# A decoder trunk on one core: three adaLN chunks summed through a fold on VectorE, with fewer steps in three units

## The chip, the cores and the metric

The kernel runs on one core of a Trainium2 chip. The time is device microseconds of one execution. Three runs of the kernel before gave 2296.66, 2296.85 and 2297.17 us; the median is 2296.85. In the text PE or TensorE is the matmul engine, DVE or VectorE the vector engine, ACT or ScalarE the activation engine, POOL or GpSimd and SP or SyncE the two engines that here only issue transfers.

## The reference

A two-layer trunk for 256 tokens of width 2048. Layer 0 mixes tokens by attention with a forget bias (16 heads of 128), layer 1 by a gated convolution of width 3; each is followed by an MLP with squared ReLU. Every sub-layer is normalised, shifted and scaled, and added back through a gate. The shifts, scales and gates (adaLN) come from the vector c:

```python
c_act = jax.nn.silu(c)
for i in range(DEPTH):
    mod = c_act @ ada_w[i] + ada_b[i]
    sh_mix, sc_mix, g_mix, sh_mlp, sc_mlp, g_mlp = jnp.split(mod, N_MOD, axis=-1)
    h = modulate(rmsnorm(x, norm_mix[i]), sh_mix, sc_mix)
    ...
    x = x + g_mix[:, None, :] * mix
    h = modulate(rmsnorm(x, norm_mlp[i]), sh_mlp, sc_mlp)
    x = x + g_mlp[:, None, :] * sq_relu_mlp(h, mlp_w_up[i], mlp_w_down[i])
return rmsnorm(x, final_norm)
```

Here `ada_w` is 2 x 2048 x 12288 in float32 (201 MB), a matrix that is read once for a product with one vector.

## The kernel before, in words

**Units and pairs.** The big products are cut into units: one unit is a 2048 x 512 slab of a weight matrix, multiplied in 8 pairs of two 128-row chunks. Units 0 to 11 are q, k and v of the four groups of heads (unit u makes part u % 3 of group u // 3), units 12 to 15 are the attention's output projection, and the MLPs and the convolution follow. Each float32 operand is split into a high and a low half of the matmul's own format, and each product is three matmuls: high x high, high x low, low x high. For every pair ScalarE rounds the weights to `w_hi` (L916), and VectorE subtracts to get `w_lo` (L1444). Both halves have four buffers (`WR`). A `w_hi` may be written when TensorE has used the pair four before it (`split_used`), and TensorE waits for `w_lo` (`split_ready`). In the body of unit u, the split at place i makes the pair 8u + 4 + i, so the two split engines work half a unit ahead.

**adaLN steps.** Of each adaLN part (2048 columns) there are two chunks of 1024 columns. A chunk takes 16 steps: a tile of 128 rows x 1024 columns of `ada_w` arrives in one of four buffers `ada_raw`, by a transfer that GpSimd issues when the step four before is done, and VectorE multiplies it by one column of c and adds it to an accumulator (L1464; the first of a chunk, L1461, only multiplies). Two accumulators alternate, `acc` for even and `hb` for odd chunks. What is left is a sum over the 128 partitions, and it has two forms (`ada_sum`, L549):

- plain: 8 matmuls with 128 x 128 blocks of the accumulator as weights and a column of ones (L562), and one store of 128 x 8 (L1495);
- folded (`fold_acc`, L1476): VectorE transposes the accumulator in blocks of 32 x 32 (L1481) and reduces it to 128 x 32 (L1483); then a single matmul with the matrix `fold` gives the sums. For a gate it is L556 with a store of 32 x 32 (L1502); for a shift or scale it is L558, and its store is four instructions, one for each 32 partitions (L1491).

`FOLDED` lists the chunks of the second form.

**The order of work.** `PLAN_QKV`, made by `plan` from rows of 8 numbers, says how many steps VectorE does behind each of the 8 splits of units 0 to 15. The six chunks done there are 0 and 1 (shift of the first MLP), 2 and 5 (its scale), 3 and 4 (gate of the attention). Where a chunk ends, `sums_of` puts its sum behind the pair four places later on TensorE and its store one place after that on VectorE. The order of each engine is fixed; semaphores alone hold them together.

**The attention between.** In units 5, 8 and 11 (and in 6 for group 1) TensorE computes a group's scores (L743 to L747), VectorE takes the maxima (L1756 to L1765), ScalarE the exponentials (L1140), VectorE the reciprocal of the sums (L1769), ScalarE normalises (L1147), and TensorE turns the probabilities (L754 to L756). Scores need the low halves of q and k, which VectorE makes behind their units (L1794). From unit 12 on a finished unit is multiplied by its gate and added to the residual (L1853, L1856).

## Time and profile before

| what | value |
|---|---|
| median of 3 runs | 2296.85 us |
| profiled execution | 2296.28 us |
| its span, first to last instruction | 2294.3 us |
| mean granted TensorE clock | 0.997 of full speed |
| PE busy | 2252.3 us (98%) |
| PE weight loads busy | 1918.9 us (84%) |
| DVE busy | 1698.3 us (74%) |
| ACT busy | 1095.7 us (48%) |
| bytes moved | 615.71 MB, mean 268 GB/s |

The busy shares are means over stages with different limits. The stage of units 5 to 15 lies between about 187 and 480 us, the first MLP behind it. A busy PE is not PE at its peak, since matmuls are pipelined and their records overlap: the distance between starts is what one costs. The same holds, by about 0.09 us, for instructions of VectorE that follow at once.

### The profile page before, as it was taken

To read this page: it belongs to the slowest core of one execution; us is meant where nothing else is said; L and a number is where in the kernel's file an instruction comes from. 1 tells how busy PE (TensorE), PEld (TensorE's weight loads), DVE (VectorE), ACT (ScalarE), POOL (GpSimd) and SP (SyncE) were. 2 spreads that over 40 slices of the span, in tenths; PEclk is the share of its full clock that TensorE was granted. 3 is DMA by queue.
4 is the path that set the end of the run, shared out by engine and by line. 5 is a ranking of instruction groups with operands and counts; after the bars stand their busy time and mean duration, and the time that the engine had idled before them with its cause. 6 is when DMAs were issued, how large, how long until landed. Compare 5 with 4: busy or idle time off the path is not lost.

```text
span 2294.3 us, 30019 instructions
## 1 busy us (share of the span) xinstructions
PE 2252.3 (98%) x11688; PEld 1918.9 (84%) x11688; DVE 1698.3 (74%) x1642; ACT 1095.7 (48%) x1264; POOL 172.6 (8%) x339
## 2 busy tenths in 40 slices
PE   6999999999999999999999999999999999999998
PEld 5999998878888888888887888887888888888886
DVE  6888999968958957967977888866895555555555
ACT  4455454464435435435545444446443543543553
POOL 0001121101101101101100111100110000000000
PEclk9999999999999999999999999999999999999999
DMA  9987999959968968978966888855986556565563
GB/s 363 386 320 258 347 354 364 349 188 319 339 214 301 348 213 286 338 236 272 335 238 238 310 326 331 317 184 168 320 302 218 185 184 202 184 195 190 184 213 117
DMA packets 271812, 615.71 MB, mean 268 GB/s; under 512 B 15472, under 2 KB 15808, under 8 KB 271296
## 3 DMA queue, kind: packets, MB, share of 16 engines
q1 hardware_dynamic: 220480, 437.56, 55.6%
q0 software_dynamic: 46080, 167.79, 20.1%
q10 hardware_dynamic: 5120, 8.49, 1.1%
q8 instruction: 96, 1.57, 0.3%
q14 instruction: 36, 0.29, 0.0%
HBM read 611.66 MB, written 2.13 MB: 268 GB/s over the span
## 4 chain that ended last, share of the span: by engine, by line
PE 92%; DVE 3%; DMA 2%; issue 1%; ACT 1%; SPq 0%; ACTq 0%; DVEq 0%
PE ps L516 19%; PE ps L518 19%; PE ps L517 19%; PE ps L504 16%; PE ps L505 8%; PE ps L491 2%; PE ps L492 2%; PE ps L493 2%; DMA start_ring<-in_ada_w_dram 2%; DVE acc L1464 1%; DVE square_out L1464 0%; PE ps L596 0%; DVE h L1600 0%; PE ps L623 0%; PE ps L880 0%
## 5 line engine op out<-in xcount | busy, mean ns | idle before, releaser
L916 ACT ACTIVATE w_hi<-raw 128x1024 fp32r<-128x1024 f32 x721 | 762.6, 1060 | 961.6 <-PE ps L518 691.9
L1444 DVE TENSOR_TENSOR w_lo<-raw,w_hi 128x1024 fp32r<-128x1024 f32 x721 | 877.6, 1222 | 449.8 <-ACT w_hi L916 448.5
L504 PE MATMUL ps<-h,w_hi 128*128 128x512 f32 x1536 | 541.4, 398 | 0.0
L516 PE MATMUL ps<-w_hi,mid 128*128 128x512 f32 x1280 | 500.0, 391 | 0.0
L518 PE MATMUL ps<-w_lo,mid 128*128 128x512 f32 x1280 | 498.4, 389 | 0.0
L517 PE MATMUL ps<-w_hi,mid 128*128 128x512 f32 x1280 | 498.4, 389 | 0.0
L505 PE MATMUL ps<-h,w_lo 128*128 128x256 f32 x1536 | 430.5, 280 | 0.0
L504 PEld LDWEIGHTS ps<-h,w_hi 128*128 128x128 f32 x1536 | 288.6, 188 | 71.6 <-DVE w_lo L1444 0.6
L516 PE MATMUL ps<-w_hi,h 128*128 128x512 f32 x756 | 298.6, 395 | 6.7 <-DVE h L1600 5.3
L518 PE MATMUL ps<-w_lo,h 128*128 128x512 f32 x756 | 294.7, 390 | 0.0
L517 PE MATMUL ps<-w_hi,h 128*128 128x512 f32 x756 | 294.6, 390 | 0.0
L505 PEld LDWEIGHTS ps<-h,w_lo 128*128 128x128 f32 x1536 | 290.1, 189 | 0.2
L474 POOL DMA_DIRECT2D ada_raw<-in_ada_w_dram x320 | 169.1, 528 | 1527.6 <-DVE acc L1461 553.7
L518 PEld LDWEIGHTS ps<-w_lo,mid 128*128 128x128 f32 x1280 | 240.3, 188 | 50.2
L516 PEld LDWEIGHTS ps<-w_hi,mid 128*128 128x128 f32 x1280 | 240.3, 188 | 50.0 <-DVE w_lo L1444 0.4
L517 PEld LDWEIGHTS ps<-w_hi,mid 128*128 128x128 f32 x1280 | 240.4, 188 | 49.1
L1464 DVE SCALAR_TENSOR_TENSOR hb<-ada_raw,ca,hb 128x1024 f32<-128x1024 f32 x150 | 191.5, 1277 | 3.3 <-DMA ada_raw<-in_ada_w_dram 2.5
L1464 DVE SCALAR_TENSOR_TENSOR acc<-ada_raw,ca,acc 128x1024 f32<-128x1024 f32 x150 | 191.7, 1278 | 2.1 <-DMA ada_raw<-in_ada_w_dram 0.9
L516 PEld LDWEIGHTS ps<-w_hi,h 128*128 128x128 f32 x756 | 142.0, 188 | 39.0 <-issue 9.6
L518 PEld LDWEIGHTS ps<-w_lo,h 128*128 128x128 f32 x756 | 141.9, 188 | 30.1
L517 PEld LDWEIGHTS ps<-w_hi,h 128*128 128x128 f32 x756 | 142.1, 188 | 27.8
L491 PE MATMUL ps<-h,w_hi 128*128 128x256 f32 x512 | 148.1, 289 | 1.3 <-DVE h L1600 1.3
(246 smaller groups left out, 1801.4 us busy)
## 6 DMA issues: line engine op xcount, KB each, us to landing
ada_raw<-in_ada_w_dram POOLq DMA_DIRECT2D x320, 512.0 KB, 6.4
raw<-in_mlp_w_up_dram SPq DMA_DIRECT2D x128, 1024.0 KB, 5.3
raw<-in_mlp_w_down_dram SPq DMA_DIRECT2D x128, 1024.0 KB, 5.8
raw<-in_fox_w_in_dram SPq DMA_DIRECT2D x48, 1024.0 KB, 10.9
raw<-in_conv_w_in_dram SPq DMA_DIRECT2D x48, 1024.0 KB, 7.9
start_ring<-in_ada_w_dram SPq DMA_DIRECT2D x64, 512.0 KB, 12.2
raw<-in_fox_w_out_dram SPq DMA_DIRECT2D x16, 1024.0 KB, 10.1
raw<-in_conv_w_out_dram SPq DMA_DIRECT2D x16, 1024.0 KB, 5.1
```

The lines of the kernel that those rows point to most:

```text
L474: pool.dma_start(ada_raw[:, t % TILES, :], ada_tile(t // KC, t % KC)).then_inc(ada_arrived[t % TILES], 16)
L491: mm(o, hi[:, jc], xh, start=(k == first and j % 2 == 0), stop=False, skip_group_check=True)
L492: mm(o, hi[:, jc], xl, start=False, stop=False, skip_group_check=True)
L493: last = mm(o, lo[:, jc], xh, start=False, stop=(k == end - 1), skip_group_check=True)
L504: mm(o, hi[:, jc], both, start=(k == 0), stop=False, skip_group_check=True)
L505: last = mm(o[:, 0:T], lo[:, jc], rhs[:, k, 0, :], start=False, stop=(k == KC - 1), skip_group_check=True)
L516: mm(o, xh, hi, start=(k == first), stop=False)
L517: mm(o, xl, hi, start=False, stop=False)
L518: last = mm(o, xh, lo, start=False, stop=(k == end - 1))
L916: op(w_hi[:, e % WR], raw[:, e // 2, EK * (e % 2):EK * (e % 2 + 1)], ACT.Copy).then_inc(hi_ready, 1)
L1444: v.tensor_tensor(w_lo[:, e % WR], raw[:, e // 2, EK * (e % 2):EK * (e % 2 + 1)], w_hi[:, e % WR].bitcast(F32), ALU.subtract).then_inc(spl ...
L1464: v.scalar_tensor_tensor(slot, src, ca[:, col:col + 1], slot, ALU.mult, ALU.add).then_inc(steps, 1)
```

## The change

Chunks 0, 1 and 2 get the folded form; of the six chunks of these units only chunk 5 (the second half of the scale) stays plain. The plan takes 10 steps in place of 11 in units 6, 7 and 8, spread otherwise within the unit, and 6, 8, 8 in place of 4, 8, 7 in units 12, 13, 14. Total and order of the steps are the same: 96. Chunks end later, so sums and stores move: in pairs (unit, place) the sums go from (6, 6), (8, 2), (9, 6), (11, 1), (13, 2) to (6, 7), (8, 4), (10, 0), (11, 4), (13, 3). The sum of chunk 5 stays at (15, 2), now by a number written out. ScalarE's write and load of the second half of the first gate come one place later in unit 13.

```diff
--- before.py
+++ after.py
@@ -60,7 +60,7 @@
 A_MLP1 = A_CONV + 2 * NH
 A_END = A_MLP1 + NH
 BLK = 32
-FOLDED = [i for i, (b, _) in enumerate(ADA) if PARTS[b] in GATE or i >= A_MLP0]
+FOLDED = [i for i in range(len(ADA)) if i != A_MLP0 - 1]
 TILES = 4
 
 
@@ -88,7 +88,8 @@
 SIX = [1, 1, 1, 0, 1, 1, 1, 0]
 FIVE = [1, 1, 1, 1, 1, 0, 0, 0]
 HALF = [1, 0] * 4
-LATE = [0] * 4 + [1] * 4
+LATE = [0] * 4 + [2, 1, 2, 1]
+EVEN = [1, 1, 1, 2, 1, 1, 2, 1]
 NONE = [0] * 8
 
 
@@ -106,7 +107,7 @@
     return first, ends
 
 
-PLAN_QKV = plan([NONE] * N_START + [ELEVEN] * 7 + [LATE, DENSE, SEVEN, NONE])
+PLAN_QKV = plan([NONE] * N_START + [ELEVEN, EVEN, EVEN, EVEN, ELEVEN, ELEVEN, ELEVEN, LATE, DENSE, DENSE, NONE])
 PLAN_SLICE = plan([NONE, SIX, SIX, SIX, SEVEN, SEVEN, NONE, NONE])
 PLAN_CONV = plan([NONE, DENSE, SIX] + [HALF, DENSE, SIX] * 2 + [HALF, DENSE, [1, 1] + [0] * 6])
 
@@ -386,7 +387,7 @@
                 at_store[t] = i
             return at_sum, at_store
 
-        QKV_SUM, QKV_STORE = sums_of(PLAN_QKV)
+        QKV_SUM, QKV_STORE = sums_of(PLAN_QKV, {2 * NH + 1: (8 * U_OUT0 + 26, 8 * U_OUT0 + 27)})
         SLICE_SUM, SLICE_STORE = sums_of(PLAN_SLICE, {1: (PLAN_SLICE[1][1] + 3, PLAN_SLICE[1][1] + 4)})
         CONV_SUM, CONV_STORE = sums_of(PLAN_CONV)
 
@@ -1300,7 +1301,7 @@
             for n in range(NG):
                 residual(at(U_OUT0 + n), n, R_OUT0, 1,
                          ({4: lambda: gate_load(0, 0, 0)},
-                          {3: load_root, 4: lambda: gate_write(A_GATE0 + 1, 0, 1), 6: lambda: gate_load(0, 1, 0)}, None, None)[n],
+                          {3: load_root, 5: lambda: gate_write(A_GATE0 + 1, 0, 1), 7: lambda: gate_load(0, 1, 0)}, None, None)[n],
                          first=None if n else {0: lambda: round_probs(NG - 1), 4: lambda: round_attn(NG - 1)})
 
 
```

What moves on VectorE is shown at three places. In the rows below, line numbers of the new kernel are one higher (L1465 is L1464 of before).

VectorE in unit 7, from the end of group 1's maxima to its reciprocal, before:

```order
L1765 TENSOR_TENSOR exp_bias<-f_tok,row_max 128x8
L1464 SCALAR_TENSOR_TENSOR hb<-ada_raw,ca,hb 128x1024
L1794 SCALAR_TENSOR_TENSOR qs<-ps,qs 128x4x256
L1444 TENSOR_TENSOR w_lo<-raw,w_hi 128x1024
L1495 TENSOR_TENSOR mod<-ps,vcol 128x8
L1464 SCALAR_TENSOR_TENSOR hb<-ada_raw,ca,hb 128x1024
L1444 TENSOR_TENSOR w_lo<-raw,w_hi 128x1024
L1769 RECIPROCAL row_inv<-row_sum 128x8
```

and now:

```order
L1766 TENSOR_TENSOR exp_bias<-f_tok,row_max 128x8
L1465 SCALAR_TENSOR_TENSOR hb<-ada_raw,ca,hb 128x1024 x2
L1795 SCALAR_TENSOR_TENSOR qs<-ps,qs 128x4x256
L1445 TENSOR_TENSOR w_lo<-raw,w_hi 128x1024
L1465 SCALAR_TENSOR_TENSOR hb<-ada_raw,ca,hb 128x1024
L1445 TENSOR_TENSOR w_lo<-raw,w_hi 128x1024
L1492 TENSOR_TENSOR mod<-ps,vcol 32x8 x4
L1770 RECIPROCAL row_inv<-row_sum 128x8
```

One step more stands behind the maxima, and the store of chunk 0 is four instructions, directly ahead of the reciprocal.

VectorE from the low half of k of group 3 (unit 10's end) to that group's first row maxima in unit 11, before:

```order
L1794 SCALAR_TENSOR_TENSOR ks<-ps,ks 128x4x256
L1444 TENSOR_TENSOR w_lo<-raw,w_hi 128x1024
L1464 SCALAR_TENSOR_TENSOR acc<-ada_raw,ca,acc 128x1024
L1444 TENSOR_TENSOR w_lo<-raw,w_hi 128x1024
L1464 SCALAR_TENSOR_TENSOR acc<-ada_raw,ca,acc 128x1024 x2
L1444 TENSOR_TENSOR w_lo<-raw,w_hi 128x1024
L1464 SCALAR_TENSOR_TENSOR acc<-ada_raw,ca,acc 128x1024
L1444 TENSOR_TENSOR w_lo<-raw,w_hi 128x1024
L1502 TENSOR_TENSOR gate_parts<-ps,gate_parts 32x32
L1756 TENSOR_REDUCE row_max<-ps 128x4
```

and now:

```order
L1795 SCALAR_TENSOR_TENSOR ks<-ps,ks 128x4x256
L1445 TENSOR_TENSOR w_lo<-raw,w_hi 128x1024
L1465 SCALAR_TENSOR_TENSOR hb<-ada_raw,ca,hb 128x1024
L1445 TENSOR_TENSOR w_lo<-raw,w_hi 128x1024
L1465 SCALAR_TENSOR_TENSOR hb<-ada_raw,ca,hb 128x1024
L1482 STREAM_TRANSPOSE hb<-hb 128x1024
L1484 TENSOR_REDUCE acc_part<-hb 128x32
L1462 TENSOR_SCALAR acc<-ada_raw,ca 128x1024
L1445 TENSOR_TENSOR w_lo<-raw,w_hi 128x1024
L1465 SCALAR_TENSOR_TENSOR acc<-ada_raw,ca,acc 128x1024
L1445 TENSOR_TENSOR w_lo<-raw,w_hi 128x1024
L1757 TENSOR_REDUCE row_max<-ps 128x4
```

The transpose and reduction of chunk 3 now stand within this stretch; before they stood ahead of it (with the last step of the chunk before them). Between the maxima of group 2 in unit 8 and this low half of k there are 29 steps and one fold in both orders: chunk 3's before, chunk 2's now. Of the 29 steps two are the first of a chunk before, one now, and the stretch holds two plain stores before and two stores of four instructions now.

VectorE in unit 12, from the first step behind the split of pair (13, 0) to the w_lo of pair (13, 4), before:

```order
L1464 SCALAR_TENSOR_TENSOR acc<-ada_raw,ca,acc 128x1024
L1444 TENSOR_TENSOR w_lo<-raw,w_hi 128x1024
L1464 SCALAR_TENSOR_TENSOR acc<-ada_raw,ca,acc 128x1024
L1444 TENSOR_TENSOR w_lo<-raw,w_hi 128x1024
L1464 SCALAR_TENSOR_TENSOR acc<-ada_raw,ca,acc 128x1024
L1481 STREAM_TRANSPOSE acc<-acc 128x1024
L1483 TENSOR_REDUCE acc_part<-acc 128x32
L1853 TENSOR_TENSOR scratch<-ps,gate 128x1024
L1856 TENSOR_TENSOR xr<-xr,scratch 128x2x512
L1444 TENSOR_TENSOR w_lo<-raw,w_hi 128x1024
L1461 TENSOR_SCALAR hb<-ada_raw,ca 128x1024
L1444 TENSOR_TENSOR w_lo<-raw,w_hi 128x1024
```

and now:

```order
L1465 SCALAR_TENSOR_TENSOR acc<-ada_raw,ca,acc 128x1024 x2
L1445 TENSOR_TENSOR w_lo<-raw,w_hi 128x1024
L1465 SCALAR_TENSOR_TENSOR acc<-ada_raw,ca,acc 128x1024
L1445 TENSOR_TENSOR w_lo<-raw,w_hi 128x1024
L1465 SCALAR_TENSOR_TENSOR acc<-ada_raw,ca,acc 128x1024 x2
L1854 TENSOR_TENSOR scratch<-ps,gate 128x1024
L1857 TENSOR_TENSOR xr<-xr,scratch 128x2x512
L1445 TENSOR_TENSOR w_lo<-raw,w_hi 128x1024
L1465 SCALAR_TENSOR_TENSOR acc<-ada_raw,ca,acc 128x1024
L1482 STREAM_TRANSPOSE acc<-acc 128x1024
L1484 TENSOR_REDUCE acc_part<-acc 128x32
L1445 TENSOR_TENSOR w_lo<-raw,w_hi 128x1024
```

Two more steps stand ahead of the gated addition (`scratch<-ps,gate`), and the fold has gone from ahead of it to behind the split that follows it.

## Rows read from the trace of the kernel before

**Rows 1.** The page: busy time by engine, and the chain of waits.

```profile
PE 2252.3 (98%) x11688; PEld 1918.9 (84%) x11688; DVE 1698.3 (74%) x1642; ACT 1095.7 (48%) x1264; POOL 172.6 (8%) x339
...
PE 92%; DVE 3%; DMA 2%; issue 1%; ACT 1%; SPq 0%; ACTq 0%; DVEq 0%
```

**Rows 2.** Windows: us, busy of PE, PEld, DVE, ACT, POOL; PEclk, DMA share, GB/s.

```profile
290.00:360.00 70.00, 70.00 (x517) 66.81 (x516) 67.44 (x65) 34.26 (x52) 14.80 (x29) 1.00 0.98 367
```

**Rows 3.** Timeline, TensorE: start, us, line, op; a plain and a folded sum.

```profile
242.96 1.84 PE L562 MATMUL ps<-ones,acc 128*128 128x1 f32 x16
244.66 0.36 PE L491 MATMUL ps<-h,w_hi 128*128 128x256 f32 x1
...
756.94 0.30 PE L558 MATMUL ps<-acc_part,fold 128*128 128x32 f32 x2
```

**Rows 4.** Timeline, VectorE, units 10 and 11.

```profile
355.39 1.25 DVE L1481 STREAM_TRANSPOSE hb<-hb 128x1024 f32<-128x1024 f32 x1
...
357.81 1.22 DVE L1444 TENSOR_TENSOR w_lo<-raw,w_hi 128x1024 fp32r<-128x1024 f32 x1
358.94 0.75 DVE L1461 TENSOR_SCALAR acc<-ada_raw,ca 128x1024 f32<-128x1024 f32 x1
359.60 1.22 DVE L1794 SCALAR_TENSOR_TENSOR ks<-ps,ks 128x1024 fp32r<-128x1024 f32 x1
...
369.67 1.23 DVE L1444 TENSOR_TENSOR w_lo<-raw,w_hi 128x1024 fp32r<-128x1024 f32 x1 [0.47 <-ACT w_hi L916]
...
370.91 0.67 DVE L1756 TENSOR_REDUCE row_max<-ps 128x4 f32<-128x512 f32 x1
```

**Rows 5.** Timeline, VectorE, a folded store in the first MLP.

```profile
763.87 0.68 DVE L1491 TENSOR_TENSOR mod<-ps,vcol 32x8 f32 x4
764.58 1.28 DVE L1464 SCALAR_TENSOR_TENSOR hb<-ada_raw,ca,hb 128x1024 f32<-128x1024 f32 x1
```

**Rows 6.** Timeline, VectorE, unit 7.

```profile
247.58 1.28 DVE L1464 SCALAR_TENSOR_TENSOR hb<-ada_raw,ca,hb 128x1024 f32<-128x1024 f32 x1
...
251.15 0.16 DVE L1495 TENSOR_TENSOR mod<-ps,vcol 128x8 f32<-128x8 f32 x1
...
253.99 1.22 DVE L1444 TENSOR_TENSOR w_lo<-raw,w_hi 128x1024 fp32r<-128x1024 f32 x1 [1.49 <-ACT w_hi L916]
255.13 0.19 DVE L1769 RECIPROCAL row_inv<-row_sum 128x8 f32<-128x8 f32 x1
```

**Rows 7.** Timeline, ScalarE, unit 7.

```profile
255.36 2.88 ACT L1147 ACTIVATE scratch<-scratch,row_inv 128x128 f32<-128x128 f32 x8 [0.46 <-DVE row_inv L1769]
```

**Rows 8.** Timeline, TensorE, starts that the prediction compares with.

```profile
259.13 0.27 PE L754 MATMUL ps<-ident,scratch 128*128 128x128 f32 x1
...
351.92 0.28 PE L491 MATMUL ps<-h,w_hi 128*128 128x256 f32 x1
...
360.92 0.30 PE L743 MATMUL ps<-ks,qs 128*128 128x128 f32 x1 [0.31 <-issue]
...
382.25 0.33 PE L754 MATMUL ps<-ident,scratch 128*128 128x128 f32 x1 [0.17 <-ACT scratch L1147]
...
419.48 0.39 PE L516 MATMUL ps<-w_hi,mid 128*128 128x512 f32 x1
```

**Rows 9.** Waits of VectorE, 290 to 360 us: total, times, longest.

```profile
DVE w_lo L1444 <- ACT w_hi L916: 2.7, 2, 2.3
DVE hb L1464 <- DMA ada_raw<-in_ada_w_dram: 1.2, 3, 0.5
DVE qs L1794 <- ACT qs L1170: 0.4, 1, 0.4
```

**Rows 10.** Waits of VectorE, 401 to 408 us.

```profile
DVE w_lo L1444 <- ACT w_hi L916: 2.3, 3, 1.7
```

**Rows 11.** Timeline, VectorE, the w_lo of pair (13, 4).

```profile
415.88 1.22 DVE L1444 TENSOR_TENSOR w_lo<-raw,w_hi 128x1024 fp32r<-128x1024 f32 x1
```

**Rows 12.** Timeline, VectorE, the w_lo of pair (10, 7).

```profile
346.48 1.22 DVE L1444 TENSOR_TENSOR w_lo<-raw,w_hi 128x1024 fp32r<-128x1024 f32 x1
```

## The prediction

> **What bounds the kernel now.** I read three views, from coarse to fine. The page's engine table and its chain of waits put TensorE first: 98% busy, 92% of the chain, and the three-product matmuls fill both [rows 1]. Taken alone this says that a microsecond removed from TensorE is a microsecond won. The windows by stage correct it. All that changes lies in units 5 to 15 (about 187 to 480 us), and between 290 and 360 us TensorE is busy 70.00 of 70 us, but VectorE 67.44 of 70 and the DMA engines 98% [rows 2]. Two engines are full there, so I read third, in the timelines, who waits for whom at the points where they meet: the w_lo halves of the weights, the attention's maxima and reciprocals, and the q and k that the scores read.
>
> **What the change does to TensorE.** A plain sum is 8 matmuls of one column, recorded as 16. It starts at 242.96 and the next weight matmul starts at 244.66: 1.70 us [rows 3]. Its record is 1.84 long, so 0.14 of a record lies over its neighbour. A folded shift or scale sum is one matmul, recorded as 2 and 0.30 long; less the same overlap it costs 0.16, and I take 0.2 [rows 3]. Three chunks change form: 3 x (1.7 - 0.2) = 4.5 us less TensorE work. This is the whole possible gain, 0.2% of the kernel, apart from some tenths of waits.
>
> The Trainium skill (VectorE: DVE Perf Modes, the section on the TRN2 errata) gives a matmul max(60, 6+FD) cycles at 2.4 GHz. By that estimate the 16 records take 0.4 us and the change could save only about 1.1 us in all. The trace has 1.70 us for them and decides; the same skill's TensorE page (TensorE: Matmul & The Clock Gate, LDWEIGHTS) names the load of 128 columns, 107 ns, which the trace bears out: 16 x 0.107 = 1.71 us.
>
> **What it does to VectorE.** Per chunk it adds one transpose and one reduction, from 355.39 to the next w_lo at 357.81: 2.42 us, plus 0.1 of longer wait ahead of the transpose, 2.5 [rows 4]. An instruction followed at once by another occupies its duration less 0.09 (357.81 to 358.94 for one of 1.22 [rows 4]). The store of 8 columns becomes four of 32 partitions each: 763.87 to 764.58 is 0.71 [rows 5], where the one store of 0.16 occupies some 0.08 [rows 6]. That is +0.63. So 3.1 us per chunk, 9.4 in all. The adaLN steps (multiply-adds of 128x1024, 1.28 us each, so one per 1.2 [rows 6]) are the same 96, only later: 74 in place of 77 by the end of unit 11.
>
> **Where VectorE's work meets TensorE.** I follow four places in order, counting what stands ahead of each on VectorE before and after.
>
> First, unit 7, the second group's softmax. The maxima follow a split that waits for TensorE, so they stay where they are. From exp_bias to the reciprocal, the new order has one step more (+1.3 as the second of a pair, which waits for its predecessor's end) and the four-part store (+0.63), against 1.49 us of idle in front of a w_lo [rows 6]. That idle ends with ScalarE's w_hi, which comes earlier with TensorE, so it is absorbed. Net +0.5: the reciprocal goes from 255.13 to 255.6. The normalising on ScalarE ends 3.1 us after the reciprocal starts (255.36 + 2.88 [rows 7]), so at 258.7. TensorE turned them at 259.13 [rows 8] and would now be there at 257.6, since the first plain sum is gone. It waits about 1.0 us, and of the first 1.5 us saved 0.5 remain.
>
> Second, units 8 to 10. The maxima of unit 8 follow a 2.3 us wait for TensorE [rows 9], so lateness starts from zero there. From them to the low half of k for group 3 (359.60 [rows 4]) VectorE runs with only 2.0 us of idle left (2.7 + 1.2 + 0.4 less the 2.3 ahead of the maxima [rows 9]). Both orders have 29 steps and one fold in this stretch, since the fold of chunk 3 moves behind it and that of chunk 2 into it. What is more: two four-part stores (+1.26), a full step in place of a first one, whose spacing is 0.66 (358.94 to 359.60 [rows 4]) and not 1.20 (+0.54), and, taken as an allowance, 0.2 for steps that now stand in pairs: +2.0 us. I let the idle absorb 1.3 (the waits for ScalarE, and those for DMA once a fold has given the transfers 2.5 us). So k is 0.7 us late. And this k is awaited already: the scores of group 3 start at 360.92 after an idle of 0.31, 0.10 behind the end of this k (359.60 + 1.22); the row names only issue [rows 8], but the moment speaks for k. Hence the two further savings (2 x 1.5) only make TensorE wait longer there. They bring nothing, and the place costs +0.7.
>
> Third, unit 11, from that k to the last maxima (359.60 to 370.91 [rows 4]). Now the fold of chunk 3 stands inside (+2.53), a first step replaces a full one (-0.54), a pair and a gate store are gone (-0.24): +1.75, of which the idle of 0.47 ahead of the w_lo absorbs its part [rows 4]: +1.3. Behind the maxima the order is as before, and TensorE waits for the probabilities already (0.17 idle at 382.25 [rows 8]). So +1.3 goes straight to the end.
>
> Fourth, units 12 and 13. VectorE waits for ScalarE three times, 2.3 us [rows 10], so lateness is zero again. Two steps more come ahead of the gated addition and the fold goes behind it: +0.15, less the 0.6 of the two shorter waits. Then fold and a full step stand ahead of the w_lo that starts at 415.88 [rows 11]: 2.53 + 0.54 - 0.45 = +2.6, so it ends 1.22 + 2.6 later, near 419.7, where TensorE wanted it at 419.48 [rows 8]. I take +0.3. What queues behind the later fold, one sum on TensorE, is due only after that pair. The gate's write and load on ScalarE's queue move back one split each, some 3 us; it is read only by the gated addition two units on, and costs nothing. Elsewhere a w_lo ends some us ahead of its pair. The nearest before the scores is in unit 10: it starts at 346.48 and ends at 347.7 [rows 12], 4.2 us before TensorE starts its pair at 351.92 [rows 8]. Lateness of about 2.7 and TensorE's gain of 3.0 exceed that by 1.5, a wait which only takes a part of the one at the scores.
>
> Sum: -0.5 + 0.7 + 1.3 + 0.3 = +1.8 us. The profiled execution took 2296.28 us (span 2294.3 and 2.0 around it), so it would take 2298.1; the median of the runs shown is 0.57 higher, so I predict 2298.6 us.
>
> **Bounds.** Each place has two ends. First: -1.5 (reciprocal in time) to +0.5 (the idle absorbs only half of the 2.0). Second: -3.0 (all lateness absorbed and k early enough) to +2.0. Third: 0 to +1.75. Fourth: -0.2 (the fold hidden, its sum one pair later) to +1.0 (2.6 + 0.6 if the short waits absorb nothing, against a cover of 2.4, 419.48 less 417.10). Together -4.7 to +5.3, the ends being unlikely together.
>
> **Rivals.**
> A. TensorE is the bound and keeps all it saves: -4.5, 2292.4 us. For it: the chain of waits, where these 70 us show as matmuls, and TensorE busy 70.00 of 70. Against it: the scores' and the probabilities' waits in rows 8. The Trainium skill (Perfetto Trace Analysis, Identifying the Most-Contended Engine) would side with it: one improves the engine with the highest occupancy first.
> B. VectorE has more give than I count, in the DMA waits and in the spacing of pairs: the second place costs nothing and gives 1.5 back, the third costs 0.5. -0.5 - 1.5 + 0.5 + 0.3 = -1.2, 2295.7 us. For it: the idle of 2.0 us; against it, 0.98 of DMA share.
> C. Slower: VectorE as the bound from unit 8 to 11 absorbs nothing, because ada_raw lands no earlier at a DMA share of 0.98 [rows 2], so that each microsecond put on it arrives at the end: 2.0 at the scores, 1.75 at the last maxima, then 1.0 at unit 13, and nothing gained in unit 7: +4.8, 2301.6 us. It decides from the point at which lateness at the scores passes the 0.7 above.
> D. The moved work lies under other cover and TensorE's gain and new waits cancel: 2296.9 us.
>
> **How the numbers follow.** Forecast 0.50, D 0.10, B 0.17, A 0.11, C 0.12. Its own range: 2297 to 2300.5. The range for 8 in 10 leaves out most of A and the outer half of C: 2293.6 to 2301.4. A difference of 0.2%, 4.6 us, is about what a measurement of this kernel can tell. A ends just inside it even in full, so faster 0.04; C passes it in two thirds of its cases, slower 0.08; within, 0.88.
>
> **What would show it.** Right: scores of group 3 start about where they did (361 us, less 0.5, plus 0.7), behind an idle of 2 to 3 us instead of 0.31; the idle before the last turning of probabilities grows from 0.17 to over 1 us; in unit 7 a new wait of 0.9; one of some tenths at 419 to 420; TensorE's sums at about 0.2 us each; stores of 0.7. Wrong: no idle on TensorE at these places and a span 4 us shorter (A); or lateness of VectorE that reaches the out units beyond 2 us, with w_lo awaited pair by pair (C).

## The result, and the profile after

The changed kernel takes 2302.47 us in the median (17 runs, 2299.29 to 2304.49) where the kernel before took 2297.82 on the same chip (17 runs). The ratio is 1.0022, with an interval of 1.0015 to 1.0028: 5.1 us slower, 3.4 to 6.4. The forecast was +1.8 us with 2301.4 as the end of its range. The direction was right, the size was not, and the outcome that the prediction gave 0.88, no measurable change, did not come. The interval is 1.5 us to each side, where the prediction had taken 4.6 us for what a measurement can tell. The profiled execution took 2300.36 us, the fourth shortest of the 17; its span is 2298.5 us, 4.2 more than before.

The page after: busy times, and the chain of waits. All line numbers are one higher than before.

```profile
PE 2248.7 (98%) x11646; PEld 1914.7 (83%) x11646; DVE 1707.2 (74%) x1657; ACT 1095.1 (48%) x1264; POOL 172.6 (8%) x339
...
PE 86%; DVE 7%; issue 3%; ACT 2%; DMA 1%; SPq 0%; DVEq 0%; ACTq 0%
```

Against [rows 1], TensorE has lost 3.6 us of busy time (in which 1.6 us of slower matmuls, below, count against it) and VectorE has gained 8.9, near the 4.5 and 9.4 of the working. The chain runs along VectorE more often: TensorE's share of it fell from 92% to 86%, and VectorE's rose from 3% to 7%. These shares follow one path and are no prices: 6% of the span is 138 us, and the change cost 4.

To place the 4.2 us, I put the starts of the same instructions of both kernels beside each other, counted from the start of pair (5, 0), which lies at 187.48 us before and 188.48 after; the 1.0 ahead of it is in the start-up, which the change does not touch (13 of the 14 kernels of the experiments had it at 187.1 to 187.7, one at 188.66). Behind (15, 3) the two differ by 0.12 us.

| start of | before | after | difference |
|---|---|---|---|
| pair (7, 4) | 72.88 | 72.46 | -0.42 |
| maxima of group 2 | 102.46 | 102.04 | -0.42 |
| low half of k, group 3 | 172.12 | 173.20 | +1.08 |
| scores of group 3 | 173.44 | 174.53 | +1.09 |
| pair (11, 2), behind them | 178.02 | 180.69 | +2.67 |
| maxima of group 3 | 183.43 | 186.00 | +2.57 |
| turning of group 3 | 194.77 | 197.52 | +2.75 |
| pair (13, 5) | 234.71 | 237.78 | +3.07 |
| pair (15, 3) | 274.50 | 277.56 | +3.06 |

Two steps stand out: 1.5 us from the maxima of group 2 to the low half of k, and 1.6 us inside the scores. Beside the second stands a third on VectorE, 1.5 us more from k to the maxima. The first is VectorE's. Its timeline after, ahead of k, and its waits from 290.6 to 361.7 us (total, times, longest):

```profile
358.01 1.22 DVE L1445 TENSOR_TENSOR w_lo<-raw,w_hi 128x1024 fp32r<-128x1024 f32 x1
360.36 1.28 DVE L1465 SCALAR_TENSOR_TENSOR hb<-ada_raw,ca,hb 128x1024 f32<-128x1024 f32 x1 [1.14 <-DMA ada_raw<-in_ada_w_dram]
361.68 1.22 DVE L1795 SCALAR_TENSOR_TENSOR ks<-ps,ks 128x1024 fp32r<-128x1024 f32 x1
```

```profile
DVE w_lo L1445 <- ACT w_hi L917: 1.2, 1, 1.2
DVE hb L1465 <- DMA ada_raw<-in_ada_w_dram: 1.1, 1, 1.1
```

The small waits of before [rows 9] are gone, as the prediction let them go. But the transfers are not ahead of VectorE: the last step ahead of k waits 1.14 us for its tile, more than any DMA wait before (0.5). The DMA share of 290 to 360 us is 0.96, about as full as in [rows 2]:

```profile
290.00:360.00 70.00, 68.75 (x501) 64.57 (x499) 68.08 (x69) 34.58 (x53) 14.77 (x28) 1.00 0.96 351
```

The second is TensorE's. First its timeline at the scores, then the windows around them (busy of PE, PEld, DVE, ACT, POOL; PEclk, DMA share, GB/s):

```profile
363.00 0.30 PE L744 MATMUL ps<-ks,qs 128*128 128x128 f32 x1 [3.50 <-issue]
...
363.36 0.27 PE L747 MATMUL ps<-nf,sel 128*128 128x128 f32 x1
363.48 0.28 PE L748 MATMUL ps<-causal,ident_r 128*128 128x128 f32 x1
...
364.61 0.41 PE L744 MATMUL ps<-ks,qs 128*128 128x128 f32 x1
364.82 0.41 PE L745 MATMUL ps<-ks,qs 128*128 128x128 f32 x1
```

```profile
363.00:366.00 3.00, 3.00 (x17) 3.00 (x18) 3.00 (x3) 0.00 (x0) 0.47 (x1) 0.60 1.02 386
366.00:369.40 3.40, 3.40 (x26) 3.40 (x26) 3.33 (x4) 0.00 (x0) 0.58 (x2) 0.85 1.03 375
369.40:372.00 2.60, 2.60 (x13) 2.09 (x13) 2.60 (x4) 0.00 (x0) 0.53 (x1) 1.00 0.88 344
```

TensorE stands still for 3.50 us, where it stood 0.31 before [rows 8]. Right behind the idle the granted clock falls to its lower level, 1.2 GHz, for 3.4 us: two 128x128 matmuls that stood 0.12 us apart (363.36, 363.48) stand 0.21 apart (364.61, 364.82). From their first matmul to the next pair the scores take 6.2 us in place of 4.6. The prediction had the idle (2 to 3 us) and did not ask what it does to the clock.

Of the other signs that it named, the following rows of after bear three out: the wait of 0.93 in unit 7, the folded sum of 0.30, a wait of 0.28 at pair (13, 4), and four-part stores of 0.68. The fourth is missing: there is no idle ahead of the last turning (386.00), since TensorE itself came late.

```profile
246.82 0.30 PE L559 MATMUL ps<-acc_part,fold 128*128 128x32 f32 x2
...
259.65 0.33 PE L755 MATMUL ps<-ident,scratch 128*128 128x128 f32 x1 [0.93 <-ACT scratch L1148]
...
386.00 0.27 PE L755 MATMUL ps<-ident,scratch 128*128 128x128 f32 x1
...
423.37 0.50 PE L517 MATMUL ps<-w_hi,mid 128*128 128x512 f32 x1 [0.28 <-DVE w_lo L1445]
```

```profile
255.77 0.68 DVE L1492 TENSOR_TENSOR mod<-ps,vcol 32x8 f32<-32x8 f32 x4
256.48 0.20 DVE L1770 RECIPROCAL row_inv<-row_sum 128x8 f32<-128x8 f32 x1
```

### The profile page after: what moved, and what is told of

The parts are those of the page before. It is cut to its first block, busy times and chain, and to the rows that moved or that the text cites. A ratio compares the mean times of both kernels' runs of the same rounds, so it can differ in the third digit from the quotient of the medians.

```text
span 2298.5 us, 29942 instructions
## 1 busy us (share of the span) xinstructions
PE 2248.7 (98%) x11646; PEld 1914.7 (83%) x11646; DVE 1707.2 (74%) x1657; ACT 1095.1 (48%) x1264; POOL 172.6 (8%) x339
## 4 chain that ended last, share of the span: by engine, by line
PE 86%; DVE 7%; issue 3%; ACT 2%; DMA 1%; SPq 0%; DVEq 0%; ACTq 0%
PE ps L517 18%; PE ps L519 18%; PE ps L518 18%; PE ps L505 15%; PE ps L506 8%; PE ps L492 2%; PE ps L493 2%; PE ps L494 2%; DVE acc L1465 1%; DVE hb L1465 1%; DMA start_ring<-in_ada_w_dram 1%; DVE w_lo L1445 1%; DVE square_out L1465 0%; PE ps L597 0%; ACT w_hi L917 0%
## 5 line engine op out<-in xcount | busy, mean ns | idle before, releaser
L1465 DVE SCALAR_TENSOR_TENSOR hb<-ada_raw,ca,hb 128x1024 f32<-128x1024 f32 x150 | 191.6, 1278 | 3.6 <-DMA ada_raw<-in_ada_w_dram 2.7
L1465 DVE SCALAR_TENSOR_TENSOR acc<-ada_raw,ca,acc 128x1024 f32<-128x1024 f32 x150 | 191.7, 1278 | 3.1 <-DMA ada_raw<-in_ada_w_dram 1.7
## 6 DMA issues: line engine op xcount, KB each, us to landing
raw<-in_fox_w_in_dram SPq DMA_DIRECT2D x48, 1024.0 KB, 10.2
```

The source lines that it names most:

```text
L1465: v.scalar_tensor_tensor(slot, src, ca[:, col:col + 1], slot, ALU.mult, ALU.add).then_inc(steps, 1)
```

## The experiments

Ratios are to the kernel before on the same chip, with their intervals; 0.1% is 2.3 us. The interval of one ratio is about 2 us to each side, so differences of one or two microseconds are read from the starts in the traces, which repeat far better: ahead of unit 7 the same instruction of TensorE lies within 0.05 us in nearly all of them, while what follows (15, 3), the same work in all, took 1830.6 to 1836.5 us. A trace is still one execution, and lengths of time at the lower clock differ between executions, as is shown further on; what a start says of the typical execution is checked against the ratio.

**The two halves of the change.** First the new plan with the old forms of the sums, then the new forms with the old plan.

```diff
 # plan only: after, with
-FOLDED = [i for i in range(len(ADA)) if i != A_MLP0 - 1]
+FOLDED = [i for i, (b, _) in enumerate(ADA) if PARTS[b] in GATE or i >= A_MLP0]
 # fold only: before, with
-FOLDED = [i for i, (b, _) in enumerate(ADA) if PARTS[b] in GATE or i >= A_MLP0]
+FOLDED = [i for i in range(len(ADA)) if i != A_MLP0 - 1]
```

> The changed kernel's plan of steps, places of sums and gate hooks, but chunks 0, 1 and 2 summed plainly as before. Theory (the folds and four-part stores make k late): VectorE loses one fold and 1.3 us of stores from the stretch ahead of k of group 3, k comes about 1.8 us earlier than in the kernel before relative to unit 8's maxima, the scores do not wait, no half clock; +1.3 at the last maxima is absorbed, unit 13 costs +0.3: within 0.5 us of the kernel before, some 4 to 5 us under the changed one. Rival (the plan itself, which moves the fold of chunk 3 and two steps behind the scores, is what costs): 2 us or more over the kernel before.

> The kernel before with chunks 0, 1 and 2 folded, the plan of steps untouched. Theory: in unit 7 the probabilities come in time, -0.9; two folds and the stores now stand in the stretch ahead of k of group 3, which comes 2.5 us late, TensorE idles some 4 to 5 us there and runs at half clock behind it, +1.6; the last maxima and unit 13 cost nothing more. Sum about +3 us over the kernel before, as the changed kernel has. Rival (TensorE is the bound, fewer matmuls win): 3 to 4.5 us under the kernel before.

Plan only: 1.0000 (0.9991 to 1.0009), (15, 3) at 274.48, as before (274.50). The plan costs nothing; it even brings k of group 3 forward, to 170.59. Fold only: 1.0060 (1.0043 to 1.0076), (15, 3) at 287.42, 12.9 us late where 3 were expected. The trace says why: three idles of 1.9 to 2.8 us on TensorE, and two stretches at the lower clock of 10.2 and 6.8 us, the second from 369.70 on. The timeline's idles, and the window of the first stretch:

```profile
237.39 0.30 PE L743 MATMUL ps<-mid 128*128 128x128 f32 x1 [1.51 <-DVE mid L1782]
...
283.45 0.30 PE L743 MATMUL ps<-ks,qs 128*128 128x128 f32 x1 [2.75 <-DVE mid L1782]
...
368.91 0.22 PE L556 MATMUL ps<-fold,acc_part 128*32 128x32 f32 x2 [1.91 <-DVE acc_part L1483]
371.92 0.45 PE L743 MATMUL ps<-ks,qs 128*128 128x128 f32 x1 [2.79 <-issue]
```

```profile
284.40:294.60 10.20, 10.20 (x42) 9.52 (x41) 5.51 (x5) 0.00 (x0) 1.97 (x4) 0.50 0.97 336
```

So the plan's fewer steps are what keeps the folds cheap, and a large part of the 12.9 us is the lower clock: 17 us of it cost TensorE up to 8.5 us (an estimate).

**The folds one by one.** On the new plan, chunk 0 alone is folded anew, then 0 and 1; the changed kernel is the third step.

```diff
-FOLDED = [i for i in range(len(ADA)) if i != A_MLP0 - 1]
+FOLDED = [i for i in range(len(ADA)) if i not in (1, 2, A_MLP0 - 1)]   # chunk 0
+FOLDED = [i for i in range(len(ADA)) if i not in (2, A_MLP0 - 1)]      # chunks 0 and 1
```

> The changed kernel with chunk 0 folded and chunks 1 and 2 plain as before (before's forms of 3, 4 and on stay folded). With the plan alone (no new fold) the pair (15,3) started 274.5 us after (5,0), as before; with all three folds 277.6. Theory (two engines take turns; TensorE's saving of chunk 0 lies ahead of unit 7's turning, where 0.4 to 0.5 of it remains, and the rest of the order is the plan's): k and scores of group 3 as in the plan-only kernel, no idle ahead of the scores, (15,3) at 274.1, total 0.4 us under before. Rival 1 (every new fold costs about 1 us, TensorE's saving is lost in waits wherever VectorE gets 3.1 us more): (15,3) at 275.5, +1. Rival 2 (TensorE bound where no fold is moved ahead of k): -1.5, (15,3) at 273.0.

> The changed kernel with chunks 0 and 1 folded and chunk 2 plain. Chunk 1's fold stands ahead of the maxima of unit 8, where VectorE waits 2 to 4 us for ScalarE anyway; only its four-part store (+0.6) lies between those maxima and the low half of k. Theory (what hurts is chunk 2's fold, 2.5 us between the maxima of group 2 and k of group 3, where nothing is idle): k at 170.6 + 0.6 - 0.4 = 170.8, scores at about 171 with no idle over 0.5 us and no stretch at the low clock; the last maxima are VectorE's and come at 183.0 - 0.4 + 0.6 = 183.2; (15,3) at 274.5, total as before within 0.5 us. Rival (each fold costs alike): +2, (15,3) at 276.5. Rival (TensorE bound once k is in time): -2, (15,3) at 272.6.

| folded anew | k, group 3 | scores | maxima 3 | (15, 3) | ratio |
|---|---|---|---|---|---|
| none | 170.59 | 172.79 | 183.04 | 274.48 | 1.0000 (0.9991 to 1.0009) |
| 0 | 170.33 | 172.35 | 182.79 | 274.22 | 1.0001 (0.9992 to 1.0010) |
| 0, 1 | 170.90 | 172.22 | 183.35 | 274.78 | 1.0001 (0.9992 to 1.0010) |
| 0, 1, 2 | 173.20 | 174.53 | 186.00 | 277.56 | 1.0022 (1.0015 to 1.0028) |

The expectations hold within 0.45 us at every point but one: with 0 and 1 folded the scores came at 172.22, not 171, behind an idle of 0.81. Chunks 0 and 1 together cost 0.3 us, chunk 2 costs 2.8. With 0 and 1 folded, TensorE's savings turn into idle, as these two rows of its timeline show:

```profile
359.40 0.30 PE L744 MATMUL ps<-ks,qs 128*128 128x128 f32 x1 [0.81 <-issue]
...
381.88 0.33 PE L755 MATMUL ps<-ident,scratch 128*128 128x128 f32 x1 [0.91 <-ACT scratch L1148]
```

**The clock taken out.** In the changed kernel, 12 matmuls with the identity keep TensorE at work while it waits for k.

```diff
                 else:
+                    if g == 3:
+                        pe.wait_ge(attn_ready, g)
+                        spin(4, 12)
                     pe.wait_ge(evacuated[(3 * g) % 2], (3 * g) // 2 + 1)
```

> The changed kernel, and 12 matmuls of 512 columns of the identity (2.8 us) that write a free bank of PSUM while TensorE waits for k of group 3, so that it does not stand idle for 3.5 us. Late k and a slow clock (my theory): scores of group 3 start within 0.3 us of where they start in the changed kernel, but the granted clock stays at 2.4 GHz and they take 4.7 us, not 6.3; the stage ends 1.6 us earlier, so the kernel takes about 1.6 us less than the changed one. Rival, the scores are slow because VectorE and the transfers are full at that time, whatever the clock: they still take 6.3 us and the time is unchanged or 0.3 longer.

1.0006 (0.9997 to 1.0015). The 12 matmuls, the first of the scores, VectorE's wait ahead of k, and the window of the scores:

```profile
358.26 2.88 PE L631 MATMUL ps<-ident_r 128*128 128x512 f32 x12
...
361.73 0.30 PE L747 MATMUL ps<-ks,qs 128*128 128x128 f32 x1 [0.59 <-issue]
```

```profile
359.09 1.28 DVE L1468 SCALAR_TENSOR_TENSOR hb<-ada_raw,ca,hb 128x1024 f32<-128x1024 f32 x1 [0.96 <-DMA ada_raw<-in_ada_w_dram]
```

```profile
361.70:366.50 4.80, 4.77 (x41) 4.80 (x42) 4.77 (x5) 0.00 (x0) 0.53 (x1) 1.00 1.03 394
```

The clock stays at 2.4 GHz, and (11, 2) comes at 178.91, 1.8 us earlier. But the maxima come only 0.54 earlier (185.46) and (15, 3) 0.68 (276.88): VectorE, not TensorE, sets the maxima, and the idle ahead of the last turning that the prediction named is there now, 0.91 us. This run splits the loss in the traces: without the lower clock +2.38 at (15, 3), with it +3.06. Of the 0.68 between them 0.20 are there at k already (173.00 against 173.20), ahead of the scores and of the lower clock, so at most 0.48 are the clock's. The timed runs differ by more than that, 0.0016 or 3.7 us, though their intervals just touch.

**k earlier.** The low half of k is taken one split earlier, `{6 if u == 10 else 7: lambda: low_qkv(u)}`.

> The changed kernel with the low half of k of group 3 made one split earlier in unit 10 (ahead of the w_lo of pair (11, 2), its step and what follows). Theory: k is ready 2.3 us earlier, TensorE's idle ahead of the scores falls from 3.5 to about 1.2 us, the clock stays at its upper level, and the scores end 4 us earlier. But VectorE then bounds the last maxima: they come only 0.3 us earlier, so TensorE waits some 3.5 us ahead of the turning of the probabilities and may get the half clock there. Time between 0.3 us less and 1.3 us more than the changed kernel. Rival (the scores' wait alone carries the loss): 4 us less than the changed kernel.

1.0009 (1.0000 to 1.0018). The scores start at 171.45 with no idle, but the maxima at 184.92, and the loss goes on to the turning, as expected; there the idle is 2.33 us and the clock falls instead:

```profile
383.68 0.48 PE L755 MATMUL ps<-ident,scratch 128*128 128x128 f32 x1 [2.33 <-ACT scratch L1148]
```

```profile
383.40:387.00 3.60, 3.32 (x14) 3.23 (x15) 3.31 (x3) 3.49 (x5) 1.06 (x2) 0.53 1.00 392
```

(15, 3) is at 277.88, 0.3 later than in the changed kernel. A wait removed at one point only showed the next, because the load on VectorE was the same. The ratio lies 3 us under the changed kernel's, with intervals that overlap; the traces do not show that gain.

**What a late k costs by itself.** The kernel before, its folds and plan untouched, with two reductions (then one) ahead of that k, whose results nobody uses; then the two with the 12 identity matmuls.

```diff
             def low_qkv(u):
                 un = at(u)
                 t = u % 3
+                if u == 10:
+                    for a in range(TT):          # TT = 2; range(1) in the second
+                        v.tensor_reduce(row_max[:, a, :], xr[:, a, 0:2 * NU].rearrange("p (b s) -> p b s", s=T), AX.X, ALU.max)
```

> The kernel before, with two reductions of 128x1024 (about 1.2 us each, results unused) directly ahead of the low half of k of group 3: k comes 2.4 us later and nothing else is changed. It asks what a late k costs by itself, and whether the granted clock falls behind an idle of TensorE of this length without any fold or changed plan. Theory (idle of 2.7 us ahead of the scores is followed by 3.4 us at half clock, as 2.3 and 3.5 us were, while 1.5 us was not): idle 2.7, clock 0.5 for 3.4 us from about 362, (11,2) at 178.0 + 2.4 + 1.7 = 182.1; the last maxima are VectorE's and come 2.4 later, 185.8; total +2.4 to +3. Rival (the low clock had another cause, such as the DMAs): no record below 1.0 in the stage, (11,2) at 180.4, total +2.4. Rival (VectorE has give left behind k): less than +1.5.

> The kernel before with one reduction in place of two ahead of the low half of k of group 3, so that k is 1.2 us late. Theory (idles of 1.5 us and less were never followed by a low clock in this case, those of 2.3 us and more always): idle 1.5 at the scores, clock 1.0, (15,3) at 275.7, total +1.2. Rival (the clock falls here too): half clock for 3.4 us or more and (15,3) at 277.4 or later.

> The kernel before with k of group 3 made 2.4 us late by two reductions, as in the late-k kernel, and 12 identity matmuls on TensorE ahead of those scores, which keep it at work while it waits. The late-k kernel had an idle of 2.64 us at the scores, then 10.2 us at half clock, and (15,3) 7.1 us later than before. Theory (2.4 of the 7.1 are the lateness itself, the other 4.7 are the low clock that follows the idle): no record below 1.0 in the stage, scores no earlier than in the late-k kernel, (15,3) at 274.5 + 2.4 to 2.7 = 277.0, total +2.5. Rival (the 7.1 comes from VectorE or the DMAs, thrown out of step by the reductions): (15,3) at 280 or later in spite of a clock of 1.0.

| k late by | idle at the scores | lower clock | (15, 3) later by | ratio |
|---|---|---|---|---|
| 1.19 (one) | 1.50 | none | 1.19 | 1.0014 (1.0005 to 1.0023) |
| 2.33 (two) | 2.64 | 10.2 us | 7.08 | 1.0021 (1.0010 to 1.0031) |
| 2.42 (two, identity matmuls) | none | none | 2.58 | 1.0012 (1.0003 to 1.0021) |

The row of the scores with one reduction, with two, and the windows behind the latter, at 0.51, and at the same place with the identity matmuls, at 1.00:

```profile
362.06 0.30 PE L743 MATMUL ps<-ks,qs 128*128 128x128 f32 x1 [1.50 <-issue]
```

```profile
363.23 0.36 PE L743 MATMUL ps<-ks,qs 128*128 128x128 f32 x1 [2.64 <-issue]
```

```profile
363.20:373.50 10.30, 10.27 (x44) 9.94 (x45) 8.21 (x7) 0.00 (x0) 2.12 (x4) 0.51 0.78 266
```

```profile
363.20:373.50 10.30, 10.30 (x67) 9.29 (x66) 9.55 (x11) 1.06 (x1) 2.11 (x4) 1.00 0.81 268
```

In these traces lateness alone passes to the end one to one (0.22 of the 2.58 lay ahead of unit 7 in that execution already), and the lower clock adds 4.5 to 4.7 us. The timed runs show less between the last two rows, 0.0009 or 2.1 us with intervals that overlap, so 4.5 is the price in one execution and the typical one stays open. The expectation of the two was too low, since it took the 3.4 us of the changed kernel for the length of such a stretch. That the length is not fixed by the length of the idle is shown; what sets it is not.

**The clock in the other executions.** The mean granted clock of the timed executions is on record too; 0.001 of it is 4.6 us at half clock, worth at most 2.3 us (an estimate). The means also hold 6.8 or 10.2 us of lower clock in the start-up and some 4 to 7 at the end of the kernel, which all 16 traces have.

| kernel | executions | mean of the clock | of them under 0.996 |
|---|---|---|---|
| before (beside the first four runs) | 29 | 0.9969 | 1 |
| changed | 17 | 0.9952 | 10 |
| changed, identity matmuls | 11 | 0.9968 | 0 |
| k late by one reduction | 11 | 0.9965 | 2 |
| k late by two | 8 | 0.9952 | 6 |
| k late by two, identity matmuls | 11 | 0.9970 | 0 |

The profiled execution of the changed kernel has 0.996. So most of its executions, ten of 17, spend more time at the lower clock than the trace shows, and the identity matmuls take that away: 0.0016 is 7.4 us of it, at most 3.7 us of time, which is the difference of the two ratios. How much of it reaches the end is not shown: the ten executions under 0.996 took 2302.6 us in the mean, the other seven 2301.5. With one reduction the two go together: the five executions at 0.995 and 0.996 took 2302.1 us in the mean, the six at 0.997 and 0.998 took 2298.5. So the "none" of that row is shown for the profiled execution alone, and its ratio, 3.2 us in place of 1.19, fits executions that lost the clock too. Where in the kernel they lost it no trace shows.

**Less on VectorE ahead of the maxima.** If the loss is VectorE's load in units 8 to 11, all three folds should be affordable with that load elsewhere. The light kernel has 10 steps in units 6 to 11 and 9 in unit 12, chunk 3's fold behind the last maxima, and k one split earlier. In unit 7 the reciprocal stands ahead of the store, and ScalarE writes the first gate half at the start of unit 12 (these two edits are not shown).

```diff
-LATE = [0] * 4 + [2, 1, 2, 1]
+LATE = [0, 1, 1, 1, 2, 1, 2, 1]
+LIGHT = [1, 1, 2, 2, 1, 1, 1, 1]
+SOFT = [1, 1, 1, 0, 2, 2, 2, 1]
-PLAN_QKV = plan([NONE] * N_START + [ELEVEN, EVEN, EVEN, EVEN, ELEVEN, ELEVEN, ELEVEN, LATE, DENSE, DENSE, NONE])
+PLAN_QKV = plan([NONE] * N_START + [ELEVEN, LIGHT, EVEN, EVEN, EVEN, EVEN, SOFT, LATE, DENSE, DENSE, NONE])
...
-                first, extra = {7: lambda: low_qkv(u)}, {}
+                first, extra = {6 if u == 10 else 7: lambda: low_qkv(u)}, {}
```

> The changed kernel, all three folds, but with VectorE's load moved out of the stretch that ends at the last maxima: 10 adaLN steps in each of units 6 to 11 and 9 in unit 12; chunk 3 ends, and is folded, behind the maxima of unit 11, its sum at (11,6), store at (11,7), ScalarE's write of the gate at the start of unit 12; the low half of k of group 3 one split earlier; in unit 7 the reciprocal ahead of the store and one step less between maxima and reciprocal. Theory (the changed kernel loses only because VectorE is full between the maxima of groups 2 and 3, and because the long idles there drop TensorE's clock): no idle over 1 us at the scores or the last turning, no low clock in 190 to 480 us, TensorE keeps what the sums save but some 0.5 in unit 7, (15,3) at 270.9 to 271.5, total 3 us under before. Rival (the last turning is bound by ScalarE and the DMAs, or the load moved to unit 12 comes out there as waits for w_lo of unit 13): (15,3) at 274 or later, no gain.

The four that follow differ from it in the steps of units 12 to 15 (and ScalarE writes the second gate half at (13, 7) and loads it at (14, 1)):

```diff
-LATE = [0, 1, 1, 1, 2, 1, 2, 1]      # then DENSE, DENSE, NONE
+LATE = [0, 1, 1, 1, 2, 1, 1, 0]      # then DENSE, DENSE, [1, 1] + [0] * 6
+LATE = [0, 0, 1, 0, 2, 2, 1, 1]      # then DENSE, [1, 1, 1, 1, 2, 1, 2, 1], NONE
+LATE = [0, 0, 1, 0, 2, 2, 1, 1]      # then DENSE, [1, 1, 1, 1, 2, 2, 2, 0], NONE
+LATE = [0, 0, 1, 0, 2, 2, 1, 2]      # then DENSE, [1, 1, 1, 1, 1, 2, 2, 0], NONE
```

> The light kernel (all three folds, 10 steps in units 6 to 11, chunk 3 folded behind the maxima of unit 11) with less in unit 12: 7, 8, 8, 2 steps in units 12 to 15 in place of 9, 8, 8, 0, so that chunk 4 ends and is folded at (13,1); ScalarE's write of the second gate half at (13,7), its load at (14,1). In the light kernel TensorE was 4.9 us ahead of before at group 3's last turning and gave 3.6 of it back in waits for w_lo of units 12 and 13 behind the fold of chunk 4, where VectorE was full from 398 to 436 us. Theory (VectorE's load is the bound there too): two steps less ahead of (13,0) and a fold behind the splits of (13,3) and (13,4) leave no wait at those two; slack at (14,3) was 0.8 and becomes a wait of some 0.5; (15,3) at 271.5, 3 us under before, 2293.5. Rival (the waits only move to units 13 to 15, since the total of VectorE up to (15,3) is as it was): (15,3) at 273.2 as in the light kernel, 1.3 under before.

> The light kernel with its load of units 12 to 15 laid otherwise: 7, 8, 10, 0 steps in units 12 to 15, in unit 12 as 0, 0, 1, 0, 2, 2, 1, 1, in unit 14 as 1, 1, 1, 1, 2, 1, 2, 1. The kernel with 2 steps in unit 15 had held the lead up to unit 14, (13,5) at 232.2 us after (5,0) against 234.7 before, and lost it at (15,2), where TensorE's plain sum of chunk 5 waited 4.64 us for the steps that now stood behind it, with 10.2 us at half clock after. Theory (that wait was only the misplaced end of chunk 5): no idle over 1.2 us between 190 and 480 us, clock 1.0, (13,5) at 231 to 232, (15,3) at 271.5 to 272.5, that is 2 to 3 us under before. Rival (VectorE's total is the bound, so the waits come back as w_lo of pairs (14,3) to (15,3)): (15,3) at 273.2 or later, no more than the 1.3 of the light kernel.

> The second light kernel (7, 8, 10, 0 steps in units 12 to 15) with the last step of chunk 5 one place earlier: unit 14 as 1, 1, 1, 1, 2, 2, 2, 0. In the second light kernel (13,5) came at 229.4 us after (5,0), 5.3 ahead of before, and all was lost again at (15,2), where the plain sum of chunk 5 waited 4.02 us for the last step, which VectorE did behind the gated addition and the w_lo of (15,3), and 6.8 us at half clock followed. Theory (the three folds save TensorE's 4.5 us, and only VectorE's order decides what is left): the last step ends at 269 us after (5,0), in time for the sum; the w_lo of (15,3) ends 1 us late; no idle over 1.5 us, clock 1.0; (15,3) at 271.5 to 272, 2.5 to 3 under before. Rival (VectorE has too much to do up to (15,3) in any order): an idle over 2 us at (15,2) or (15,3), (15,3) at 274 or later, no gain.

> The same with one step moved from unit 14 to the end of unit 12: unit 12 as 0, 0, 1, 0, 2, 2, 1, 2, unit 14 as 1, 1, 1, 1, 1, 2, 2, 0. The w_lo of (13,6), behind chunk 4's fold, was 0.82 us late in the second light kernel. Theory: it becomes some 1.5 late, later waits none or under 1 us, (15,3) at 271.5 to 272.5. Rival: as above.

| units 12 to 15 | scores 3 | turning 3 | (13, 0) | (13, 5) | (15, 3) | ratio |
|---|---|---|---|---|---|---|
| before | 173.44 | 194.77 | 220.71 | 234.71 | 274.50 | |
| 9, 8, 8, 0 (light) | 168.54 | 189.85 | 216.96 | 233.42 | 273.21 | 0.9998 (0.9988 to 1.0007) |
| 7, 8, 8, 2 | 168.55 | 189.85 | 218.59 | 232.19 | 278.88 | 1.0019 (1.0010 to 1.0028) |
| 7, 8, 10, 0 (second light) | 168.57 | 189.87 | 215.75 | 229.38 | 275.38 | 1.0011 (1.0002 to 1.0020) |
| the same, last step earlier | 168.54 | 189.85 | 215.77 | 229.37 | 274.44 | 1.0002 (0.9993 to 1.0011) |
| 8, 8, 9, 0 | 168.54 | 189.84 | 215.73 | 231.33 | 271.91 | 0.9995 (0.9986 to 1.0004) |

Up to the last turning all five are 4.9 us ahead of before: TensorE keeps the 4.5 us of the three sums, and the 0.31 and 0.17 that it had waited at the scores and the turning. The rest is where that lead goes, and four of the five expectations for (15, 3) were missed; only the last version's, 271.5 to 272.5, held. In the light kernel, w_lo of unit 13 behind chunk 4's fold is late. With 2 steps in unit 15 I erred: the last of them stands behind the split of pair (15, 5), and the plain sum of chunk 5 stands at (15, 2), so TensorE waited 4.64 us, and the clock fell for 10.2 us, from 1.4 us before that wait ended. The second light kernel held 5.3 us at (13, 5) and lost it at the same sum:

```profile
461.66 0.58 PE L566 MATMUL ps<-ones,hb 128*128 128x1 f32 x4 [4.02 <-DVE hb L1466]
```

```profile
462.80:469.60 6.80, 6.80 (x20) 5.64 (x21) 2.12 (x2) 0.06 (x1) 0.00 (x0) 0.50 1.03 385
```

With its last step earlier the waits shrank to 0.81, 1.47 and 1.52, but the clock fell at the end of the third, for 3.4 us, and the expectation (271.5 to 272) was missed:

```profile
462.05 0.79 PE L520 MATMUL ps<-w_hi,mid 128*128 128x512 f32 x1 [1.52 <-DVE w_lo L1446]
```

```profile
462.00:465.40 3.40, 3.35 (x8) 2.68 (x9) 3.40 (x3) 0.43 (x2) 0.00 (x0) 0.51 0.93 322
```

The last version, with 8 steps in unit 12, is the best found. Its longest idles and a window over units 11 to 13:

```profile
417.55 0.22 PE L560 MATMUL ps<-fold,acc_part 128*32 128x32 f32 x2 [0.79 <-DVE acc_part L1485]
418.59 0.50 PE L520 MATMUL ps<-w_hi,mid 128*128 128x512 f32 x1 [0.82 <-DVE w_lo L1446]
...
459.17 0.50 PE L520 MATMUL ps<-w_hi,mid 128*128 128x512 f32 x1 [0.53 <-DVE w_lo L1446]
```

```profile
360.00:430.00 70.00, 68.39 (x323) 56.60 (x322) 67.44 (x65) 35.29 (x57) 12.66 (x24) 1.00 0.96 352
```

It is 2.6 us ahead of before at (15, 3) and its span is 2291.2 us against 2294.3, with all three folds. Whether the whole kernel is faster the timed runs leave open (0.9995, 0.9986 to 1.0004); faster than the changed kernel it is, by intervals that do not meet.

## Why the prediction was wrong

**TensorE's and VectorE's prices were right.** VectorE's busy time grew by 8.9 us against 9.4. The light kernels show the 4.5 in full as a lead (4.9 with the 0.31 and 0.17 of waits), so the whole possible gain was sized rightly.

**First place, right.** -0.42 at (7, 4) against -0.5, with the wait of 0.93 against 1.0.

**Second place, wrong in two ways, and this is the step that failed.** "I let the idle absorb 1.3 (the waits for ScalarE, and those for DMA once a fold has given the transfers 2.5 us)." This left +0.7 for the place. Relative to group 2's maxima k came 1.50 us later in the changed kernel, and 1.30 in the run with identity matmuls, where VectorE has the same instructions up to k. The waits of this stretch fell from 2.0 us to 1.1 and 0.96, so 0.9 to 1.0 was absorbed, not 1.3, and the added work comes out at 2.3 to 2.4 (lateness and absorbed wait together, an estimate), not 2.0. What is left of the waits is one, for a tile, where no single DMA wait before was over 0.5 [rows 9]. Two steps stand in a row there and one follows; at a DMA share of 0.96 to 1.05 the transfers gave no room. Rival C had said this of ada_raw.

The second way is a missing term. The prediction made the wait at the scores longer on purpose ("the two further savings (2 x 1.5) only make TensorE wait longer there. They bring nothing"). They brought an idle of 3.50 us, and with it the lower clock: 1.6 us more inside the scores, of which at most 0.48 reach (15, 3) in the profiled executions. No rival had it.

The Trainium skill has the rule that was left unused (TensorE: Matmul & The Clock Gate, Part 1: The HAM clock gate): an idle array falls to 1.2 GHz, and activity brings 2.4 GHz back. The traces here agree with both directions: behind the idle of 3.50 us the windows read 0.60 and 0.85, and 1.00 from 369.40 on.

**Third place, right.** From k to the last maxima +1.15 without the clock (2.03 less 0.88), against +1.3; with it 1.49.

**Fourth place, right.** +0.35 at (15, 3) (2.38 less 2.03), against +0.3; in the changed kernel 0.49.

The sum as it came out without the clock is -0.42 + 1.30 + 1.15 + 0.35 = +2.38, and in the changed kernel -0.42 + 1.50 + 1.49 + 0.49 = +3.06, where the forecast had 1.8. To it comes 1.0 in the start-up of this execution, which the change does not touch. So +3.1 us are explained place by place; the ratio gives +5.1 (3.4 to 6.4). The 0.3 to the lower end and more are not explained by this trace. The clock record points to the missing term: ten of the 17 executions have a lower mean clock than the profiled one, and with the identity matmuls both the clock and 3.7 us of the ratio come back. Which idles did it there, and what reached the end, stays open.

**The rivals.** A is refuted: the changed kernel and its variants with identity matmuls and with the earlier k had TensorE's savings and no gain. B wanted 1.5 us back at the second place, which cost 1.3 to 1.5, and D's sum of nothing came out as 3.1 or more. C had the right mechanism at the second place, and was too dear everywhere: 2.0 against 1.30, 1.75 against 1.15, 1.0 against 0.35 (without the clock). It gave nothing for unit 7, where 0.42 was gained. Its total of +4.8 lies near the measured 5.1 by luck: its three terms are 2.0 us too large together, and it had no term for the clock. With C at 0.12, the case that VectorE and the DMAs have no give was rated too low beside a row that showed them at 67.44 of 70 us and 0.98. The 0.88 for no measurable change rested on a sum of terms that all were waits, and took none of them to have a cost beyond its own length.

## What to carry to other kernels

When a change unloads one full engine by loading another full one, count what stands between two points at which they meet, and do not credit an idle in full unless what ends it (here a transfer) is shown to have room. When the sum lengthens an idle of TensorE from tenths to more than 2 us, price the matmuls behind it at half the clock for some microseconds and name who returns the loss: in the traces here the wait for VectorE's maxima gave back 1.1 of 1.6 us, while behind a late k alone next to nothing came back. One trace can show a short stretch where most executions had more, so read the clock of all of them. Work moved off the critical stretch has to land somewhere: five placements of the same 96 steps, all 4.9 us ahead at one point, ended from 2.6 us ahead to 4.4 behind.

## What the runs showed of the hardware

In the profiled executions, in the stage of units 5 to 15, the granted clock fell at idles of TensorE of 2.33, 2.64, 2.75, 3.50, 4.02 and 4.64 us, each time, for 3.4, 10.2, 10.2, 3.4, 6.8 and 10.2 us; so a longer idle did not mean a longer stretch. The fall came between 1.4 us before the end of the idle (4.64) and 1.2 us behind it (4.02). At single idles of 1.50 and 1.51 us it stayed at 2.4 GHz. It did fall at the last of three idles of 0.81, 1.47 and 1.52 us within 12 us, and behind one of 1.91 us and a sum, 0.6 us into the next idle of 2.79. Over all executions the mean clock of the kernel with the idle of 1.50 us ran from 0.995 to 0.998, so what one trace shows of such an idle need not hold in the next. Twelve identity matmuls, 2.9 to 3.0 us of work without use, held the clock in both kernels where they were tried, and none of their 22 executions had a mean under 0.996.
